# Gated recurrence in a two-part transformer kernel: convolved columns projected first, gate matmuls between the tiles, the elementwise chain in two groups, the output projection by block

## The chip, the core and the metric

The kernel runs on one core of a Trainium2 chip. A core has TensorE (PE in the profile) for matmuls, VectorE (DVE), ScalarE (ACT) and GpSimd (POOL) for elementwise work, and SyncE (SP), which here only issues the loads of weights. Each engine has its own instruction stream; they meet at semaphores. Matmul results go to eight PSUM banks of 128 x 512 float32 values, and a bank can be written again only when another engine has drained it. The metric is the device time of one whole execution in microseconds (us), as the median over the runs.

## The reference, cut to what matters

The model takes 512 tokens of width 1024 through two blocks of two layers each. The change is in one stage, the mixer of the last layer, a gated linear recurrence. `hn` is the normalised input, 512 x 1024.

```python
def rglru_mixer(hn, w_in, conv_w, conv_b, w_a, b_a, w_x, b_x, lam, w_out):
    gate, xr = jnp.split(hn @ w_in, 2, axis=-1)                 # 512 x 1024 each
    xr = (causal_dwconv(xr, conv_w) + conv_b).astype(f32)       # 4 taps
    xb = xr.reshape(b, t, LRU_BLOCKS, LRU_BLOCK)                # 8 blocks of 128
    r = jax.nn.sigmoid(jnp.einsum('btni,nij->btnj', xb, w_a) + b_a)
    i = jax.nn.sigmoid(jnp.einsum('btni,nij->btnj', xb, w_x) + b_x)
    log_a = -LRU_C * r * jax.nn.softplus(-lam)
    a = jnp.exp(log_a)
    u = jnp.sqrt(-jnp.expm1(2.0 * log_a)) * (i * xr)
    _, hs = lax.associative_scan(_linear_combine, (a, u), axis=1)
    y = jax.nn.gelu(gate) * hs
    return y @ w_out
```

Behind it follow the residual, a norm and the convolutional feed-forward layer.

## The kernel before, in words

The kernel is a sequence of stages; the order of the instructions on each engine is written out by hand, and stage 9 is the one of the change. A plan made ahead of the code hands out the eight banks in turn (`plan.take`) and the four weight slots in two pairs (`plan.chunk`): a weight chunk of 1024 x 512 is loaded into one slot of a pair, and its rounded copy goes into the other. The product is made in three matmuls of rounded float32 (`product`): high by high, high by low, low by high. For that ScalarE rounds a chunk in two halves (`round_chunk`), VectorE subtracts the rounded half from the raw one (`rest_of_chunk`), and both have to be done before TensorE uses that half (semaphore `split`). SyncE may load into a slot again only when TensorE has finished the last tile that used it (`c.freed`).

In stage 9 channels lie on the partitions and the 512 tokens in the free dimension. The input projection has 2048 output columns, in four chunks of four tiles of 128 columns; a tile fills one bank with 24 matmuls. The kernel before projects the columns of `gate` first (chunks 0 and 1), which ScalarE takes out of the banks with a Gelu, and the columns of `xr` next (chunks 2 and 3), which VectorE takes out with the convolution (`conv`: one operation and three more, lines 2361 and 2364). The matmuls with the block-diagonal gate weights, two for each of eight tiles, stand behind all of it (line 1926). ScalarE then makes the 16 sigmoids (1347, 1350). After that comes the chain, tile by tile: product i times xr on VectorE (2782), exp, tanh and square on ScalarE (1360, 1362, 1366), the root's argument on VectorE (2788), the root on ScalarE (1370), the product with it on GpSimd (863), the scan over tokens on VectorE (2795), the product with the gate (2797), its rounding on ScalarE (1373) and the rest on VectorE (2802). The output projection waits for all eight tiles:

```python
                pe.wait_ge(signal("lru_y").sem, signal("lru_y").next(pe, KD))
                linear("lru_out")
```

Its stationary operands are XT (rounded) and XH (rest), which were the input of the stage as well: so the chain can't write XT while the input is still being projected.

The names of buffers in the rows: `ring` are the four weight slots, `big` the working area (gate, xr, i, the gate weights w, the squares q), `XT` and `XH` the turned input and its rest, `lnp` a buffer of 2 x 1024 values per partition, `st` and `chan` small tables.

## Time and profile before

| | us |
|---|---|
| median of 3 runs | 3577.34 (3575.35 to 3580.39) |
| profiled execution, its own time | 3585.4 |
| its span, first to last instruction | 3583.6 |
| TensorE busy | 3174.9 (89%) |
| VectorE busy | 2314.3 (65%) |
| ScalarE busy | 1611.3 (45%) |
| GpSimd busy | 412.0 (11%) |

The clock granted to TensorE was 0.936 of the full one in the mean over the span. In the rows, a time at the start is counted from the first instruction; "x8" counts instructions; square brackets, or the last column, hold the idle time of the engine just before, with what ended it. Matmuls overlap, so a duration of 0.39 us is longer than the distance between two starts. In the rows of the trace a float32 gate matmul appears as two records.

### The profile page before, as it was taken

The numbers are of one execution on the slowest core, as the hardware profiler recorded it, in microseconds if no ns is written. First come the engines' busy times: TensorE is split into PE (matmuls) and PEld (weight loads), VectorE is DVE, ScalarE is ACT, GpSimd is POOL, SyncE is SP. The second block draws the span as 40 slices with busy tenths as digits, with TensorE's granted clock in tenths as the row PEclk, the third lists the DMA queues.
The fourth block names the chain that finished last, engine by engine and source line by source line (L and its number), as shares of the span: only waits on it lengthen the run. The fifth ranks groups of instructions, "written<-read, shape, count | busy, mean of one in ns | idle before, by whom it ended". The sixth has DMA issues, their size and how long they took to land.

```text
span 3583.6 us, 40435 instructions
## 1 busy us (share of the span) xinstructions
PE 3174.9 (89%) x15107; PEld 2476.2 (69%) x15107; DVE 2314.3 (65%) x2594; ACT 1611.3 (45%) x1831; POOL 412.0 (11%) x290
## 2 busy tenths in 40 slices
PE   8678699999969999699999969867799998679998
PEld 6456577777758768567767658656678887468886
DVE  2465588888862576778888746466467743657763
ACT  2454277777742353577777632222132213522221
POOL 0000222222220000222222120001100000010000
PEclk9889899999989889799999979888899999889999
DMA  7200499999952003699999844200022222212222
GB/s 262 79 1 12 186 356 346 351 355 357 355 189 94 1 24 113 241 344 349 362 357 361 333 110 99 70 1 1 6 89 94 94 99 78 82 53 94 94 94 82
DMA packets 173509, 597.54 MB, mean 167 GB/s; under 512 B 25491, under 2 KB 74691, under 8 KB 123971
## 3 DMA queue, kind: packets, MB, share of 16 engines
q1 hardware_dynamic: 139552, 539.92, 41.1%
q0 software_dynamic: 23472, 51.42, 4.1%
q10 hardware_dynamic: 10355, 4.42, 0.5%
q8 instruction: 87, 1.43, 0.2%
q14 instruction: 43, 0.35, 0.0%
HBM read 581.01 MB, written 48.23 MB: 176 GB/s over the span
## 4 chain that ended last, share of the span: by engine, by line
PE 76%; DVE 11%; DMA 5%; ACT 3%; issue 3%; POOL 1%; DVEq 0%; SPq 0%; ACTq 0%; POOLq 0%
PE bank L1420 22%; PE bank L1422 21%; PE bank L1421 21%; PE bank L1829 2%; DMA ring<-w_gate 2%; PE bank L1525 2%; PE bank L1602 1%; PE bank L1499 1%; PE bank L1395 1%; DVE st L2093 1%; DVE st L2096 1%; PE bank L1622 1%; DVE big L2090 1%; PE bank L1516 1%; ACT ring_rounded L1021 1%
## 5 line engine op out<-in xcount | busy, mean ns | idle before, releaser
L1421 PE MATMUL bank<-ring_rounded,big_rounded 128*96 128x512 f32 (+1 forms) x1648 | 651.4, 395 | 0.0
L1964 DVE TENSOR_TENSOR ring_rounded<-ring,ring_rounded 128x2048 fp32r<-128x2048 f32 (+2 forms) x128 | 282.5, 2249 | 501.4 <-ACT ring_rounded L901 501.3
L2275 DVE TENSOR_TENSOR ring_rounded<-ring,big_rounded 128x2048 fp32r<-128x2048 f32 x252 | 567.3, 2288 | 42.6 <-ACT big_rounded L1021 41.4
L1021 ACT ACTIVATE big_rounded<-ring 128x2048 fp32r<-128x2048 f32 x252 | 478.0, 1918 | 61.2 <-DMA ring<-w_up 52.7
L901 ACT ACTIVATE ring_rounded<-ring 128x2048 fp32r<-128x2048 f32 (+2 forms) x128 | 234.2, 1880 | 521.1 <-DMA ring<-ffn_w_up 184.8
L1420 PE MATMUL bank<-big_rounded 128*96 128x512 f32 x1008 | 401.1, 398 | 0.0
L1422 PE MATMUL bank<-big_rounded,XH_rounded 128*96 128x512 f32 x1008 | 398.4, 395 | 0.0
L2275 DVE TENSOR_TENSOR ring_rounded<-ring,ring_rounded 128x2048 fp32r<-128x2048 f32 x128 | 292.7, 2288 | 163.0 <-ACT ring_rounded L1021 154.9
L1420 PE MATMUL bank<-ring_rounded,XT_rounded 128*128 128x512 f32 (+1 forms) x864 | 340.4, 394 | 60.6 <-DVE XH_rounded L2802 46.6
L1422 PE MATMUL bank<-ring_rounded,XH_rounded 128*96 128x512 f32 (+1 forms) x944 | 377.3, 400 | 0.0
L1420 PE MATMUL bank<-XT_rounded,ring_rounded 128*128 128x512 f32 x928 | 361.3, 389 | 0.0
L1422 PE MATMUL bank<-XT_rounded,ring_rounded 128*128 128x512 f32 x928 | 361.0, 389 | 0.0
L1421 PE MATMUL bank<-XH_rounded,ring_rounded 128*128 128x512 f32 x928 | 361.0, 389 | 0.0
L1421 PEld LDWEIGHTS bank<-ring_rounded,big_rounded 128*96 128x96 f32 (+1 forms) x1648 | 272.8, 166 | 106.4 <-issue 0.5
L1021 ACT ACTIVATE ring_rounded<-ring 128x2048 fp32r<-128x2048 f32 x128 | 245.1, 1916 | 222.6 <-DMA ring<-w_gate 222.5
L1421 PE MATMUL bank<-ring_rounded,XT_rounded 128*128 128x512 f32 (+1 forms) x864 | 338.3, 392 | 0.0
L1420 PE MATMUL bank<-ring_rounded,big_rounded 128*96 128x512 f32 (+1 forms) x640 | 261.8, 409 | 15.0 <-DVE XH_rounded L2280 7.3
L1422 PE MATMUL bank<-ring_rounded,big_rounded 128*128 128x512 f32 (+1 forms) x672 | 261.8, 390 | 0.0
L1420 PEld LDWEIGHTS bank<-ring_rounded,XT_rounded 128*128 128x128 f32 x864 | 164.3, 190 | 96.0 <-DVE XH_rounded L2802 47.4
L1422 PEld LDWEIGHTS bank<-big_rounded,XH_rounded 128*96 128x96 f32 x1008 | 162.3, 161 | 71.5
L1420 PEld LDWEIGHTS bank<-big_rounded 128*96 128x96 f32 x1008 | 164.8, 164 | 66.3 <-DVE ring_rounded L2275 0.8
L1422 PEld LDWEIGHTS bank<-ring_rounded,XH_rounded 128*96 128x96 f32 (+1 forms) x944 | 166.8, 177 | 55.6 <-issue 0.3
(389 smaller groups left out, 4799.2 us busy)
## 6 DMA issues: line engine op xcount, KB each, us to landing
ring<-w_up SPq DMA_DIRECT2D x128, 1024.0 KB, 7.7
ring<-w_down SPq DMA_DIRECT2D x128, 1024.0 KB, 7.9
ring<-w_gate SPq DMA_DIRECT2D x128, 1024.0 KB, 7.3
ring<-ffn_w_up SPq DMA_DIRECT2D x44, 1024.0 KB, 6.8
ring<-ffn_w_down SPq DMA_DIRECT2D x10, 2048.0 KB, 7.8
ring<-ret_gdn_w_in SPq DMA_DIRECT2D x8, 2048.0 KB, 13.1
expert_rows<-lnp POOLq DMA_DIRECT2D x1, 12288.0 KB, 39.2
ring<-odd_w_qkv SPq DMA_DIRECT2D x6, 2048.0 KB, 8.1
```

Source lines behind the costliest of these rows:

```text
L901: act.activation(one_pass(hi(c)[:, ks, :]), raw(c)[:, ks, :], ACT.Copy).then_inc(rounded[c.pair], 1)
L1021: act.activation(one_pass(expert_hi(j)), expert_raw(j), ACT.Copy).then_inc(signal("half_rounded").sem, 1)
L1395: ins = pe.transpose(ps(u)[:, t * P:(t + 1) * P], src[:, t, i * P:(i + 1) * P], ident)
L1420: pe.matmul(dst, x_hi, y_hi, start=first, stop=False)
L1421: pe.matmul(dst, x_hi, y_lo, start=False, stop=False)
L1422: return pe.matmul(dst, x_lo, y_hi, start=False, stop=last)
L1499: ins = pe.matmul(ps(v)[:, :], buf["QKT"][r, g % 2, 0, t * P:(t + 1) * P], buf["QKT"][r, g % 2, 1, :], start=True, stop=True)
L1516: ins = pe.transpose(ps(v)[:, kt * P:(kt + 1) * P], buf["p"][(i - 2) % 3][:, o, kt * P:(kt + 1) * P], ident)
L1525: ins = pe.matmul(ps(v)[:, 0:c["dv"]], buf["WT"][:, (i - 3) % 2, o, kt, :], c["v"]((i - 3) // T, o, kt), start=(kt == 0), stop=(kt == T - 1))
L1829: ins = pe.matmul(ps(u)[:, i * P:(i + 1) * P], lhsT[:, 2 * q + i, :], rhs[:, 2 * q + i, :], start=True, stop=True)
L1964: dve.tensor_tensor(one_pass(w), w, parts(hi(c)[:, ks, :]), ALU.subtract).then_inc(split[c.pair], 1)
L2275: dve.tensor_tensor(one_pass(expert_raw(j)), expert_raw(j), parts(expert_hi(j)), ALU.subtract).then_inc(signal("half_split").sem, 1)
```

## The change

- The weight columns are loaded in the order 2, 3, 0, 1, so that chunks 0 and 1 are now the columns of xr and chunks 2 and 3 those of gate.
- The gate matmuls stand between tiles of the projection: those of blocks 0 and 1 behind the first tile of chunk 1, of 2 and 3 behind its second, of 4 and 5 behind the first tile of chunk 2, of 6 and 7 behind its second. The plan of banks follows that order.
- The gate weights are loaded earlier, before the turned input is rounded.
- The chain runs in two groups, blocks 0 to 3 and 4 to 7. Its buffer r (sigmoid, tanh, root) is no longer XT but four tiles in lnp; the second group uses them again when the first has been scanned. The product with the root is on VectorE instead of GpSimd.
- Two of the gate tiles are copied out of their banks and put through the Gelu later in place, the other six go through it on the way out. Product with the gate, rounding and rest come last; the results stay in the buffers of xr and i.
- The output projection takes its stationary operands from there and waits for each block by itself in its first tile.

```diff
+LRU_GATES = {(1, 0): (0, 1), (1, 1): (2, 3), (2, 0): (4, 5), (2, 1): (6, 7)}
...
+        for i in range(4):
+            c = plan.chunk(KD, BANK, BANK)
+            us = []
+            for q in range(4):
+                us += plan.take()
+                for m in LRU_GATES.get((i, q), ()):
+                    U["lru"][m] = plan.take(2)
...
+        L_["r"] = lnp[:, :, :].rearrange("p a (b s) -> p (a b) s", b=2)
...
-                load_cols("lru_in", a["lru_w_in_2"][0], 2 * D)
+                load_cols("lru_in", a["lru_w_in_2"][0], 2 * D, order=(2, 3, 0, 1))
...
-                for m in range(KD):
-                    pool.wait_ge(signal("lru_root").sem, signal("lru_root").next(pool))
-                    pool.tensor_tensor(XT[:, m, :], XT[:, m, :], L_["i"][:, m, :], ALU.mult).then_inc(signal("lru_in").sem, 1)
...
+                def sigmoids(ms):
                     for m in ms:
+                        ur, ui = U["lru"][m]
+                        if m >= KD // 2:
+                            act.wait_ge(signal("lru_scanned").sem, signal("lru_scanned").next(act))
...
+                early, last = range(0, KD // 2), range(KD // 2, KD)
+                round_chunk(W["lru_in"][1])
+                round_chunk(W["lru_in"][2])
+                sigmoids(early)
+                act.wait_ge(signal("cvec_ready").sem, signal("cvec_ready").next(act))
+                decays(early)
+                roots(early)
+                round_chunk(W["lru_in"][3])
+                gate_tile(0, ACT.Copy)
+                sigmoids(last[0:2])
+                gate_tile(1, ACT.Copy)
+                sigmoids(last[2:4])
+                decays(last)
+                roots(last)
+                round_chunk(W["lru_out"][0])
+                for m in range(2):
+                    act.activation(L_["gate"][:, m, :], L_["gate"][:, m, :], ACT.Gelu_apprx_tanh).then_inc(signal("lru_gelu").sem, 1)
+                    act.wait_ge(signal("lru_gelu").sem, signal("lru_gelu").next(act))
+                for m in range(2, 6):
+                    gate_tile(m, ACT.Gelu_apprx_tanh)
+                for m in range(4):
+                    round_gated(m)
+                for m in range(6, 8):
+                    gate_tile(m, ACT.Gelu_apprx_tanh)
+                    round_gated(m - 2)
+                for m in range(6, 8):
+                    round_gated(m)
+                round_chunk(W["lru_out"][1])
...
+                    for q in range(4):
+                        linear_T(c, us, range(4), "rms1_T" if i == 0 else None, q)
+                        for m in LRU_GATES.get((i, q), ()):
+                            if m == 0:
+                                pe.wait_ge(signal("gates_loaded").sem, signal("gates_loaded").next(pe, 32))
+                            v = U["lru_in"][m // 4][m % 4]
+                            pe.wait_ge(drained[v.bank], v.n + 1)
+                            for j, u in enumerate(U["lru"][m]):
+                                if u.n:
+                                    pe.wait_ge(drained[u.bank], u.n)
+                                pe.matmul(ps(u)[:, :], L_["w"][:, j, m, :], L_["xr"][:, m, :], start=True, stop=True).then_inc(
+                                    full[u.bank], 1)
...
-                pe.wait_ge(signal("lru_y").sem, signal("lru_y").next(pe, KD))
-                linear("lru_out")
...
+                            if i == 0 and t == 0:
+                                pe.wait_ge(signal("lru_y").sem, signal("lru_y").next(pe))
...
+                rest_of_chunk(W["lru_in"][1])
+                for m in range(5):
+                    lru_conv(m)
+                rest_of_chunk(W["lru_in"][2])
+                for m in range(2):
+                    gated_input(m)
+                lru_conv(5)
+                for m in range(2, 4):
+                    gated_input(m)
+                for m in range(2):
+                    lru_conv(6 + m)
+                    root_argument(2 * m)
+                    root_argument(2 * m + 1)
+                for m in range(4):
+                    recurrence(m)
+                rest_of_chunk(W["lru_in"][3])
+                for m in range(4, 8):
+                    gated_input(m)
+                for m in range(4, 8):
+                    root_argument(m)
+                for m in range(4, 8):
+                    recurrence(m)
+                rest_of_chunk(W["lru_out"][0])
+                for m in range(4):
+                    gated(m)
+                for m in range(4, 8):
+                    rest_of_gated(m - 4)
+                    gated(m)
+                for m in range(4, 8):
+                    rest_of_gated(m)
+                rest_of_chunk(W["lru_out"][1])
```

First the order on TensorE around the first gate matmuls, before the change, with the semaphores each instruction waits for. L1420 to L1422 are the three matmuls of a product, L1926 is a gate matmul; this is the end of the last projected tile.

```order
L1421 MATMUL bank<-XH_rounded,ring_rounded 128x512
L1422 MATMUL bank<-XT_rounded,ring_rounded 128x512
L1926 MATMUL bank<-big 128x512 [waits bank3_drained,gates_loaded]
L1926 MATMUL bank<-big 128x512 [waits bank4_drained]
L1926 MATMUL bank<-big 128x512 [waits bank5_drained,bank4_drained]
L1926 MATMUL bank<-big 128x512 [waits bank6_drained]
L1926 MATMUL bank<-big 128x512 [waits bank7_drained,bank5_drained]
L1926 MATMUL bank<-big 128x512 [waits bank0_drained]
```

Eight more gate matmuls follow, and then the output projection. After the change the first four stand behind the fifth projected tile, with the sixth tile behind them (the product is now L1459 to L1461, a gate matmul L1970):

```order
L1460 MATMUL bank<-XH_rounded,ring_rounded 128x512
L1461 MATMUL bank<-XT_rounded,ring_rounded 128x512
L1970 MATMUL bank<-big 128x512 [waits bank0_drained,bank3_drained,gates_loaded]
L1970 MATMUL bank<-big 128x512 [waits bank1_drained]
L1970 MATMUL bank<-big 128x512 [waits bank2_drained,bank4_drained]
L1970 MATMUL bank<-big 128x512 [waits bank3_drained]
L1459 MATMUL bank<-XT_rounded,ring_rounded 128x512 [waits bank4_drained]
L1460 MATMUL bank<-XH_rounded,ring_rounded 128x512
```

So sixteen gate matmuls in one row became four groups of four, each ahead of a projected tile that now stands behind their waits.

ScalarE in the middle of the stage, before the change: L901 rounds half a chunk, L1336 is a Gelu out of a bank, L1347 and L1350 are the sigmoids.

```order
L1336 ACTIVATE big<-bank 128x512 x4
L901 ACTIVATE ring_rounded<-ring 128x2048 x2
L1336 ACTIVATE big<-bank 128x512 x4
L877 DMA big<-lru_w_a 128x8x128
L877 DMA big<-lru_w_x 128x8x128
L901 ACTIVATE ring_rounded<-ring 128x2048 x4
L1347 ACT_TABLE_LOAD
L1347 ACTIVATE XT<-bank,chan 128x512
L1350 ACTIVATE big<-bank,chan 128x512
```

After the change, the place between the first group's roots (L1373) and the second group's sigmoids (L1348, L1352); L908 rounds the fourth chunk and L1378 takes a gate tile out of its bank.

```order
L1373 ACT_TABLE_LOAD
L1373 ACTIVATE lnp<-lnp 128x512 x4
L908 ACTIVATE ring_rounded<-ring 128x2048 x2
L1378 ACTIVATE big<-bank 128x512
L1348 ACT_TABLE_LOAD
L1348 ACTIVATE lnp<-bank,chan 128x512
L1352 ACTIVATE big<-bank,chan 128x512
L1348 ACTIVATE lnp<-bank,chan 128x512
L1352 ACTIVATE big<-bank,chan 128x512
L1378 ACTIVATE big<-bank 128x512
```

The rounding of the fourth chunk, which needs its load, now stands ahead of the gate tile and the sigmoids of the second group.

VectorE at the end of the stage, before: L2795 is the scan, L2797 the product with the gate, L2802 the rest, L2028 the residual.

```order
L2795 SCALAR_TENSOR_TENSOR big<-big,XT 128x512
L2797 TENSOR_TENSOR big<-big 128x512
L2802 TENSOR_TENSOR XH_rounded<-big,XT_rounded 128x4x128
L2795 SCALAR_TENSOR_TENSOR big<-big,XT 128x512
L2797 TENSOR_TENSOR big<-big 128x512
L2802 TENSOR_TENSOR XH_rounded<-big,XT_rounded 128x4x128 x5
L2028 SCALAR_TENSOR_TENSOR X<-X,bank 128x512 x4
```

After: L2847 is the scan, L2018 the rest of the first output chunk, L2856 the product with the gate, L2861 the rest.

```order
L2845 TENSOR_TENSOR lnp<-lnp,big 128x512
L2847 SCALAR_TENSOR_TENSOR big<-big,lnp 128x512
L2018 TENSOR_TENSOR ring_rounded<-ring,ring_rounded 128x2048 x2
L2856 TENSOR_TENSOR big<-big 128x512 x4
L2861 TENSOR_TENSOR big_rounded<-big,big_rounded 128x512
L2856 TENSOR_TENSOR big<-big 128x512
L2861 TENSOR_TENSOR big_rounded<-big,big_rounded 128x512
L2856 TENSOR_TENSOR big<-big 128x512
L2861 TENSOR_TENSOR big_rounded<-big,big_rounded 128x512
L2856 TENSOR_TENSOR big<-big 128x512
L2861 TENSOR_TENSOR big_rounded<-big,big_rounded 128x512
```

The products with the gate moved from between the scans to behind all of them and behind a weight chunk's rest.

## Rows read from the trace of the kernel before

**Rows 1.** Page, costliest groups: busy, mean ns, idle before.
```profile
L1420 PE MATMUL bank<-ring_rounded,XT_rounded 128*128 128x512 f32 (+1 forms) x864 | 340.4, 394 | 60.6 <-DVE XH_rounded L2802 46.6
```

**Rows 2.** Stretches: length; PE, PEld, DVE, ACT, POOL busy; clock; DMA share, GB/s.
```profile
2400.00:2500.00 100.00, 65.86 (x424) 59.67 (x422) 66.43 (x107) 23.59 (x42) 17.00 (x12) 0.80 0.00 1
3002.00:3089.00 87.00, 87.00 (x389) 72.14 (x387) 41.49 (x51) 27.05 (x26) 0.00 (x0) 1.00 0.26 85
3089.00:3100.00 11.00, 11.00 (x28) 4.93 (x26) 5.82 (x8) 4.22 (x5) 0.00 (x0) 1.00 0.55 191
3100.00:3155.00 55.00, 5.62 (x10) 2.12 (x9) 42.93 (x42) 40.51 (x58) 13.12 (x8) 0.56 0.00 0
```

**Rows 3.** Timeline of TensorE in the stage: start us, duration us.
```profile
3002.54 0.47 PE L1420 MATMUL bank<-XT_rounded,ring_rounded 128*128 128x512 f32 x1
...
3089.69 10.46 PE L1926 MATMUL bank<-big 128*128 128x512 f32 x24
...
3102.95 5.37 PE L1926 MATMUL bank<-big 128*128 128x512 f32 x8 [2.80 <-ACT XT L1347]
3154.90 0.79 PE L1420 MATMUL bank<-ring_rounded,XT_rounded 128*128 128x512 f32 x1 [46.58 <-DVE XH_rounded L2802]
3155.49 0.63 PE L1421 MATMUL bank<-ring_rounded,XT_rounded 128*128 128x512 f32 x1
3155.92 0.63 PE L1422 MATMUL bank<-ring_rounded,XH_rounded 128*128 128x512 f32 x1
...
3199.91 0.39 PE L1422 MATMUL bank<-ring_rounded,XH_rounded 128*128 128x512 f32 x1
```

**Rows 4.** Timeline of VectorE in the stage.
```profile
3009.54 4.49 DVE L1964 TENSOR_TENSOR ring_rounded<-ring,ring_rounded 128x2048 fp32r<-128x2048 f32 x2
...
3062.83 0.81 DVE L2361 TENSOR_SCALAR big<-bank,chan 128x512 f32<-128x512 f32 x1
3063.67 2.32 DVE L2364 SCALAR_TENSOR_TENSOR big<-bank,chan,big 128x511 f32<-128x511 f32 x3
...
3123.72 2.31 DVE L2795 TENSOR_TENSOR_SCAN big<-big,XT 128x512 f32<-128x512 f32 x1 [2.66 <-POOL XT L863]
3126.06 1.58 DVE L2797 TENSOR_TENSOR big<-big 128x512 f32<-128x512 f32 x1
...
3129.36 1.22 DVE L2795 TENSOR_TENSOR_SCAN big<-big,XT 128x512 f32<-128x512 f32 x1
3130.61 0.69 DVE L2797 TENSOR_TENSOR big<-big 128x512 f32<-128x512 f32 x1
...
3151.25 3.60 DVE L2802 TENSOR_TENSOR XH_rounded<-big,XT_rounded 128x512 fp32r<-128x512 f32 x5
```

**Rows 5.** Timeline of ScalarE in the stage.
```profile
3032.75 3.72 ACT L901 ACTIVATE ring_rounded<-ring 128x2048 fp32r<-128x2048 f32 x2 [7.48 <-DMA ring<-lru_w_in]
...
3046.43 0.60 ACT L1336 ACTIVATE big<-bank 128x512 f32<-128x512 f32 x1 [4.84 <-PE bank L1422]
...
3056.47 3.72 ACT L901 ACTIVATE ring_rounded<-ring 128x2048 fp32r<-128x2048 f32 x2 [9.44 <-DMA ring<-lru_w_in]
...
3110.75 1.28 ACT L1360 ACT_TABLE_LOAD   x1
3112.04 0.72 ACT L1360 ACTIVATE big<-XT,st 128x512 f32<-128x512 f32 x1
```

**Rows 6.** ScalarE's instructions by line, 3079 to 3156: busy us, mean ns, idle before.
```profile
L1350 ACT ACTIVATE big<-bank,chan 128x512 f32<-128x512 f32 x8 | 5.5, 687 | 0.6 <-PE bank L1926 0.4
L1360 ACT ACTIVATE big<-XT,st 128x512 f32<-128x512 f32 x8 | 5.7, 710 | 0.0
L1362 ACT ACTIVATE XT<-XT,st 128x512 f32<-128x512 f32 x8 | 5.8, 721 | 0.3
L1366 ACT ACTIVATE big<-big 128x512 f32<-128x512 f32 x8 | 5.0, 629 | 0.3
```

**Rows 7.** DMA issues, 2960 to 3220: size, median us to landing.
```profile
ring<-lru_w_in SPq DMA_DIRECT2D x4, 2048.0 KB, 8.1
```

More of the change, by code:

```diff
@@ L358, in build @@
         U["rms1_T"] = plan.take(KD)
-        plan_linear("lru_in", 2 * D)
-        U["lru"] = [plan.take(2) for _ in range(KD)]
+        W["lru_in"], U["lru_in"], U["lru"] = [], [], [None] * KD
+        for i in range(4):
[5 more added lines that the diff above has]
+                    U["lru"][m] = plan.take(2)
+            plan.freed[c.slot] = ("bank", us[-1])
+            W["lru_in"].append(c)
+            U["lru_in"].append(us)
         plan_linear("lru_out", D)
@@ L1446, in linear_chunk, with linear_T @@
                     ins.then_inc(full[u.bank], 1)
-            def linear_T(c, us, tiles, turned=None):
+            def linear_T(c, us, tiles, turned=None, only=None):
                 for q, (u, m) in enumerate(zip(us, tiles)):
+                    if only is not None and q != only:
+                        continue
                     if u.n:
@@ L1924, in _ @@
+                for i, (c, us) in enumerate(zip(W["lru_out"], U["lru_out"])):
+                    for t, u in enumerate(us):
                         if u.n:
                             pe.wait_ge(drained[u.bank], u.n)
-                        pe.matmul(ps(u)[:, :], L_["w"][:, j, m, :], L_["xr"][:, m, :], start=True, stop=True).then_inc(
-                            full[u.bank], 1)
-                pe.wait_ge(signal("lru_y").sem, signal("lru_y").next(pe, KD))
-                linear("lru_out")
+                        for kk in range(KD):
+                            if t == 0 and kk % 4 == 0:
+                                pe.wait_ge(split[c.pair], 2 * c.nth - 1 + kk // 4)
+                            if i == 0 and t == 0:
+                                pe.wait_ge(signal("lru_y").sem, signal("lru_y").next(pe))
+                            tok = slice(t * P, (t + 1) * P)
+                            ins = product(ps(u)[:, :], L_["xr"][:, kk, tok], L_["i"][:, kk, tok], hi(c)[:, kk, :], raw(c)[:, kk, :], kk == 0, kk == KD - 1)
+                        ins.then_inc(full[u.bank], 1)
```

105 lines of the change are left out of this document (44 added, 61 removed).

## The prediction, made before the changed kernel was run

> **What bounds the kernel now.** I read the page first. TensorE is busy for 3174.9 of 3583.6 us, so only a stretch in which it stands still can give much. The costliest groups show one: the first matmul of a product whose stationary side is XT waited 46.6 us for VectorE's line 2802, the last step of the recurrence [rows 1]. Next the table of stretches: from 3002 to 3100 TensorE is never idle and the clock is granted in full (1.00, the 2.4 GHz level), while in 3100:3155 it has 5.62 us of work [rows 2]. The timeline then gives the frame of the stage: the input projection starts at 3002.54 and ends at 3089.69, the gate matmuls run until 3108.3, and the output projection runs from 3154.90 to 3200.3, where the next stage takes over [rows 3]. These 197.8 us are the stretch that the change can alter. TensorE's own work in it is much shorter; the rest is the elementwise chain (sigmoid, exp, tanh, square, root, scan), which begins only after the last projected tile.
>
> **What TensorE must do, as one number.** A tile of 24 matmuls takes (3089.69 - 3002.54)/16 = 5.45 us, 0.227 a matmul. A gate matmul leaves two records, 24 records take 10.46 us, so one costs 0.87 us and sixteen 13.95 us [rows 3]. The output projection has 192 matmuls, 43.5 us; it took 45.4 because its first ones started 0.43 us apart (the low level, 1.2 GHz, after the long wait) [rows 3]. Without any wait the stage takes 87.15 + 13.95 + 43.5 = 144.6 us, 53.2 less than now. That is the most the change can give, since it removes no matmul.
>
> **The change, part by part.** The order of the weight chunks (xr columns first), the gate matmuls between tiles and the two groups only move work. So the question is whether each wait in the new TensorE order is met in time. I write TensorE's undisturbed times in the clock of this trace: xr tiles 0 to 3 done at 3024.3, tile 4 at 3029.8, gates 0 and 1 at 3033.3, tile 5 at 3038.7, gates 2 and 3 at 3042.2, tiles 6 and 7 at 3053.1; gate column tile 0 at 3058.5, gates 4 and 5 at 3062.0, column tile 1 at 3067.4, gates 6 and 7 at 3070.9, column tiles 2 and 3 at 3081.8, the last chunk at 3103.6, the output projection at 3147.2.
>
> First group. VectorE is done with the second chunk's rest at 3014.0 [rows 4]; a convolution is 0.81 + 2.32 us, with its gaps 3.2 [rows 4], so tiles 0 to 3 are convolved by 3027.5 and tile 4 by 3033.0. Gates 0 and 1 need tiles 0 and 1 (3020.4) at 3029.8: 9 us to spare. ScalarE rounds the third chunk, whose load starts when TensorE has finished the first, as now: 3032.75 to 3036.4 [rows 5]. A table load is 1.28 [rows 5] and a sigmoid 0.69, 0.72 with its gap [rows 6]; sigmoids 0 and 1 end at 3040.5, those of 2 and 3 at 3043.3. The bank of the last matmul of gate 3 wants the first sigmoid (3038.4) at 3041.3: met by 3 us. Exp, tanh and square are 2.03 us a tile [rows 6]. The third square waits for VectorE, which first convolves tile 6 (full at 3047.6); that costs ScalarE about 1.5 us, and the four roots end at 3058.3. The multiplication by the root moves from GpSimd to VectorE, where this trace doesn't show it: a product of the same shape takes 0.69 us, and 1.58 while GpSimd was working [rows 4]. I take 0.69, since GpSimd has nothing left to do here, and 1.22 for the scan for the same reason (2.31 beside GpSimd) [rows 4]. Four tiles then end at 3065.5.
>
> Second group, the tight place. The load of the fourth chunk can start at 3053.1. A load takes 8.1 us in the median [rows 7]; the present fourth one took 10.0 (from the end of the second chunk at 3046.4 to 3056.47) [rows 5], beside the two gate weight loads. Those now go out before the transposed tiles and have some 30 us until the first gate. So ScalarE rounds from 3061.3 to 3065.1, copies column tile 0, loads a table and finishes the sigmoids of tile 4 at 3068.4. TensorE wants the last of these banks at 3070.9: 2.5 us to spare, 0.6 if the load takes 10.0. Roots of the second group end at 3086.4, scans at 3092.4. All that is under the last two chunks, on which TensorE works until 3103.6.
>
> Tail. The rounding of the first output chunk (load from 3081.8) ends on ScalarE at 3093.7, VectorE's rest of it at 3096.9. Gated products and rests go at 0.72 each on VectorE (five rests in 3.60) [rows 4]. The in-place Gelu isn't in the trace; between 0.60 (Gelu out of a bank) and 0.72 (exp) I take 0.63 [rows 5, 6]. By that order lru_y 0 to 7 come at 3100.5, 3102.0, 3103.4, 3104.8, 3106.3, 3107.0, 3107.7 and 3108.4. TensorE now asks for them one block at a time, at 3103.6 and every 0.68 us after: the fifth and the last are just met, some tenths late. I put 0.4 us on that. The last output chunk arrives at 3111.7 and is split by 3118, wanted at 3125.4.
>
> Nothing else is on the path: lnp is free between the squares and the last load, GpSimd loses only its eight products, and the residual and the next stage follow the end of the output projection as before.
>
> ScalarE loads seven tables from the first sigmoid on, where it loaded five. The trace shows such a load at 3110.75 for 1.28 us and the next exp at 3112.04, at once [rows 5]; so I count 1.28. The Trainium skill, in ScalarE: Activation LUTs (What ACT_TABLE_LOAD costs), adds some 1.38 us of drain to each switch. By that rule, an estimate, three switches make the first group 4.1 us later, and with those of the second the last lru_y about 5 us: the time would be some 3530 us. The trace speaks against it.
>
> **Sum.** Before 197.8, after 144.6 + 0.4 = 145.0: 52.8 us less. The profiled execution took 3585.4 us (1.8 around its span) and would take 3532.6. The median of the runs is 3577.3, 8.1 lower; there the same difference gives 3524.5 us.
>
> **Rivals.**
> *Late elementwise work* (0.13). VectorE's operations cost what they cost beside GpSimd (1.58 for 0.69, 2.31 for 1.22 [rows 4]), or loads take 10 us. Loads alone push the tail by 2 to 3 us; the dear operations add 16 x 0.9 = 14 us in the tail and 4 x 2 = 8 before it. TensorE would stand for 10 to 20 us ahead of or inside the output projection: 3535 to 3545. For it: most slacks are a few us. Against it: GpSimd is idle here.
> *It does not do what it says* (0.04). The second group stays behind the last projected tile because one engine's order holds it. Half of the present wait of 46.6 us [rows 1] stays, 23 us: 3548.
> *Slower* (0.03). TensorE waits shortly at the sixteen gate matmuls between the tiles, and the clock stays at the low level. At 0.43 instead of 0.227 us [rows 3], 576 projection matmuls cost 117 us more, the gate matmuls up to 14: 3655. It decides from 52.8/0.203 = 260 matmuls at that level. For it: where TensorE works in short pieces, the granted clock is 0.80 in the mean [rows 2]. Against it: from 3002 to 3100 it changes bank every 5.4 us, then every 0.9, at 1.00 [rows 2], and by my times it never waits there. TensorE: Matmul & The Clock Gate, in the Trainium skill (A second HAM failure mode), warns of small pauses between groups of matmuls when banks are cycled; by that rule the time would be this rival's.
>
> **Chances and range.** 0.80 for the forecast (its own range 3517 to 3532: the runs of one kernel spread by 5 us, and each slack may be missed by a little). Faster by over 0.2% (7 us, about what a measurement of this kernel can tell) holds in all cases but the last: 0.95; within 0.2% 0.02, for a mixture of the last two; slower 0.03. The range takes in most of the late case: 3514 to 3543.
>
> **What would show it.** Right: no idle time of TensorE over 1 us between the first tile and the end of the output projection, a stretch of 145 us at clock 1.00; GpSimd without products; VectorE's scans at 1.22. Wrong: idle time at the third gate column tile (banks of the sigmoids of tile 4), or at the first output tile behind lru_y; or a clock under 1.00 between tiles.

## The result, and the profile after

| | before | changed |
|---|---|---|
| median of the first four runs, us | 3576.35 (3564.93 to 3580.39) | 3529.33 (3524.35 to 3544.72) |
| medians of the later rounds, us | 3581.14 (11 runs) | 3531.99 (6 runs) |
| profiled execution, its own time, us | 3585.4 | 3544.7 |
| span | 3583.6 | 3543.0 |
| TensorE busy | 3174.9 | 3184.5 |
| GpSimd busy | 412.0 | 409.1 |

The change is faster: the ratio is 0.9876 (95% interval 0.9841 to 0.9911), and in the five later rounds 0.9842 (0.9819 to 0.9865). The difference of the medians is 47.0 us, later 49.1 us; the ratios of the medians alone would be 0.987 and 0.986. The prediction was 52.8 us and 3524.5.

GpSimd's total hardly fell, though its eight products (13.12 us in the fourth stretch of [rows 2]) are gone: in the stretches from 500 to 1000 and from 1500 to 2000 us, whose code the change leaves alone, the profile counts 7 us more for it in each (114.95 and 121.95, 115.22 and 122.30).

Below, "the stage" is the time from the first matmul of the input projection to the start of the last residual instruction. It went from 197.9 us (3002.54 to 3200.40) to 146.3 us (3013.32 to 3159.61), 51.6 us less. The last residual instruction before and after:

```profile
3200.40 0.69 DVE L2028 SCALAR_TENSOR_TENSOR X<-X,bank 128x512 f32<-128x512 f32 x1 [4.75 <-PE bank L1422]
```

```profile
3159.61 0.69 DVE L2082 SCALAR_TENSOR_TENSOR X<-X,bank 128x512 f32<-128x512 f32 x1 [4.75 <-PE bank L1461]
```

The whole profiled execution gained only 40.7, because this one came to the stage 10.8 us later; behind the stage both take 383 us. The later 10.8 us are the subject of experiment 8.

TensorE's timeline in the changed kernel, which answers to [rows 3]: start, duration, and in brackets the idle time ahead.

```profile
3013.32 0.47 PE L1459 MATMUL bank<-XT_rounded,ring_rounded 128*128 128x512 f32 x1
...
3078.17 3.59 PE L1970 MATMUL bank<-big 128*128 128x512 f32 x8
3081.20 0.79 PE L1459 MATMUL bank<-XT_rounded,ring_rounded 128*128 128x512 f32 x1
...
3114.26 0.39 PE L1459 MATMUL bank<-ring_rounded,big_rounded 128*128 128x512 f32 x1
...
3116.83 0.50 PE L1459 MATMUL bank<-ring_rounded,big_rounded 128*128 128x512 f32 x1 [0.37 <-DVE big_rounded L2861]
...
3118.38 0.47 PE L1459 MATMUL bank<-ring_rounded,big_rounded 128*128 128x512 f32 x1 [0.58 <-DVE big_rounded L2861]
```

From 3013.32 to 3114.26 there is no wait: 16 tiles and 16 gate matmuls in 100.9 us. The last four gate matmuls (eight records, 3.59 us) stand among the tiles. The wait of 46.6 us for line 2802 [rows 1, 3] is gone; in its place are two short waits for the rest of single blocks (line 2861), 0.37 and 0.58 us, inside the first output tile. The stretches say the same, with the columns of [rows 2]:

```profile
3013.00:3100.00 87.00, 87.00 (x360) 66.76 (x359) 64.76 (x83) 56.25 (x69) 0.00 (x0) 1.00 0.21 73
3100.00:3115.00 15.00, 15.00 (x68) 12.43 (x67) 14.56 (x16) 12.52 (x16) 0.00 (x0) 1.00 0.00 2
3115.00:3160.00 45.00, 43.56 (x190) 34.88 (x188) 19.17 (x20) 12.85 (x14) 2.20 (x6) 1.00 0.28 94
```

The clock is 1.00 throughout; GpSimd has no product left. VectorE (14.56 of 15 us) is full and ScalarE (12.52) nearly so just ahead of the output projection. That is the tail of the chain. VectorE's last four rests:

```profile
3117.54 2.87 DVE L2861 TENSOR_TENSOR big_rounded<-big,big_rounded 128x512 fp32r<-128x512 f32 x4
```

So the last lru_y (the signal that a block of the stationary operand is complete) comes at 3120.41, 107.1 us after the start of the stage, and the stage ends 39.2 us after it.

ScalarE at the place that the prediction called tight, to be read beside [rows 5]:

```profile
3073.00 3.72 ACT L908 ACTIVATE ring_rounded<-ring 128x2048 fp32r<-128x2048 f32 x2 [3.60 <-DMA ring<-lru_w_in]
3076.63 0.57 ACT L1378 ACTIVATE big<-bank 128x512 f32<-128x512 f32 x1
3077.21 1.28 ACT L1348 ACT_TABLE_LOAD   x1
3078.51 0.69 ACT L1348 ACTIVATE lnp<-bank,chan 128x512 f32<-128x512 f32 x1
3079.23 0.69 ACT L1352 ACTIVATE big<-bank,chan 128x512 f32<-128x512 f32 x1
```

It stood 3.60 us for the load of the fourth chunk. The sigmoids of tile 4 were out of their banks at 3079.20 and 3079.92. TensorE needed the first bank for its last gate matmul at about 3080.8 (six records of 0.436 us behind 3078.17) and the second for its next tile at 3081.20, so 1.6 and 1.3 us were to spare. The load had taken 8.9 us, not 8.1:

```profile
3064.04 8.94 DMA ring<-lru_w_in
```

### The profile page after: what moved, and what is told of

It is laid out like the page before. It is cut to its first block, busy times and chain, and to the rows that moved or that the text cites. A ratio compares the mean times of both kernels' runs of the same rounds, so it can differ in the third digit from the quotient of the medians.

```text
span 3543.0 us, 40440 instructions
## 1 busy us (share of the span) xinstructions
PE 3184.5 (90%) x15107; PEld 2484.9 (70%) x15107; DVE 2313.2 (65%) x2602; ACT 1615.3 (46%) x1834; POOL 409.1 (12%) x282
## 4 chain that ended last, share of the span: by engine, by line
PE 77%; DVE 10%; DMA 5%; ACT 3%; issue 3%; POOL 1%; DVEq 0%; SPq 0%; ACTq 0%; POOLq 0%
PE bank L1459 22%; PE bank L1461 21%; PE bank L1460 21%; PE bank L1870 2%; DMA ring<-w_gate 2%; PE bank L1566 2%; PE bank L1540 1%; PE bank L1643 1%; PE bank L1434 1%; PE bank L1557 1%; DVE st L2147 1%; DVE st L2150 1%; PE bank L1663 1%; DVE ring_rounded L2018 1%; ACT ring_rounded L1028 1%
## 5 line engine op out<-in xcount | busy, mean ns | idle before, releaser
L1460 PE MATMUL bank<-ring_rounded,big_rounded 128*96 128x512 f32 (+1 forms) x1712 | 675.0, 394 | 0.0
L2018 DVE TENSOR_TENSOR ring_rounded<-ring,ring_rounded 128x2048 fp32r<-128x2048 f32 (+2 forms) x128 | 282.4, 2248 | 458.4 <-ACT ring_rounded L908 458.2
L908 ACT ACTIVATE ring_rounded<-ring 128x2048 fp32r<-128x2048 f32 (+2 forms) x128 | 234.1, 1879 | 503.2 <-DMA ring<-ffn_w_up 169.0
L1459 PE MATMUL bank<-big_rounded 128*96 128x512 f32 x1008 | 401.2, 398 | 0.1
L1461 PE MATMUL bank<-big_rounded,XH_rounded 128*96 128x512 f32 x1008 | 398.2, 395 | 0.0
L1459 PE MATMUL bank<-XT_rounded,ring_rounded 128*128 128x512 f32 x928 | 362.9, 391 | 0.0
L1461 PE MATMUL bank<-XT_rounded,ring_rounded 128*128 128x512 f32 x928 | 361.0, 389 | 0.0
L1460 PEld LDWEIGHTS bank<-ring_rounded,big_rounded 128*96 128x96 f32 (+1 forms) x1712 | 283.9, 166 | 108.1 <-issue 0.3
L1461 PE MATMUL bank<-ring_rounded,XH_rounded 128*96 128x512 f32 (+1 forms) x880 | 349.9, 398 | 0.0
L1459 PE MATMUL bank<-ring_rounded,XT_rounded 128*128 128x512 f32 (+1 forms) x800 | 314.1, 393 | 14.6 <-DVE ring_rounded L2018 6.9
L1460 PE MATMUL bank<-ring_rounded,XT_rounded 128*128 128x512 f32 (+1 forms) x800 | 312.1, 390 | 0.0
L1459 PE MATMUL bank<-ring_rounded,big_rounded 128*96 128x512 f32 (+1 forms) x704 | 285.6, 406 | 14.6 <-DVE XH_rounded L2334 5.8
L1461 PE MATMUL bank<-ring_rounded,big_rounded 128*128 128x512 f32 (+1 forms) x736 | 286.4, 389 | 0.0
L1461 PEld LDWEIGHTS bank<-big_rounded,XH_rounded 128*96 128x96 f32 x1008 | 162.3, 161 | 71.5
L1459 PEld LDWEIGHTS bank<-big_rounded 128*96 128x96 f32 x1008 | 164.7, 163 | 66.3 <-DVE ring_rounded L2329 0.5
L751 POOL DMA_INDIRECT expert_rows<-big,idx x64 | 98.6, 1541 | 885.5 <-ACT big L1050 830.1
L1460 PEld LDWEIGHTS bank<-XH_rounded,ring_rounded 128*128 128x128 f32 x928 | 174.2, 188 | 37.1 <-issue 1.0
## 6 DMA issues: line engine op xcount, KB each, us to landing
expert_rows<-lnp POOLq DMA_DIRECT2D x1, 12288.0 KB, 39.2
```

The lines of the kernel that those rows point to most:

```text
L751: pool.indirect_dma_start(expert_rows, bass.IndirectOffsetOnAxis(ap=used[0:CAP, e:e + 1], axis=0), M["YE"][0:CAP, e % 2, :], None, bounds_ ...
L908: act.activation(one_pass(hi(c)[:, ks, :]), raw(c)[:, ks, :], ACT.Copy).then_inc(rounded[c.pair], 1)
L1459: pe.matmul(dst, x_hi, y_hi, start=first, stop=False)
L1460: pe.matmul(dst, x_hi, y_lo, start=False, stop=False)
L1461: return pe.matmul(dst, x_lo, y_hi, start=False, stop=last)
L2018: dve.tensor_tensor(one_pass(w), w, parts(hi(c)[:, ks, :]), ALU.subtract).then_inc(split[c.pair], 1)
```

## The experiments

Every run left a profile of its own, so the stage is read to a tenth of a microsecond, whatever the rest of the execution did. The last columns belong to experiment 8: when the stage began, and how long the attention stretch of an earlier stage took (from the last load of `odd_w_qkv` to the first of `odd_w_o`, the same code in all) at which granted clock.

| run | stage | begins | attention stretch | its clock |
|---|---|---|---|---|
| before | 197.9 | 3002.5 | 141.5 | 0.92 |
| changed | 146.3 | 3013.3 | 153.7 | 0.82 |
| 1 by block, on the kernel before | 192.9 | 3016.5 | 153.7 | 0.82 |
| 2 waits for all blocks | 153.1 | 3001.4 | 143.1 | 0.90 |
| 3 product on GpSimd | 147.9 | 2989.7 | 136.1 | 0.96 |
| 4 gates two tiles later | 154.9 | 2989.2 | 136.0 | 0.96 |
| 5 four extra copies | 149.3 | 3002.8 | 138.3 | 0.94 |
| 6 twelve extra copies | 154.2 | 3004.6 | 143.3 | 0.90 |
| 7 idle time used | 144.8 | 3005.5 | 143.3 | 0.90 |
| 8 changed, again | 146.6 | 3004.9 | 141.3 | 0.92 |
| 9 column order alone, on before | 197.9 | 2994.6 | 138.3 | 0.94 |
| 10 second group behind | 176.9 | 2994.1 | 136.1 | 0.96 |

### 1. The blockwise wait alone

```diff
-                pe.wait_ge(signal("lru_y").sem, signal("lru_y").next(pe, KD))
-                linear("lru_out")
...
+                        for kk in range(KD):
...
+                            if i == 0 and t == 0:
+                                pe.wait_ge(signal("lru_y").sem, signal("lru_y").next(pe))
```

> The kernel before, with only the output projection's wait taken apart: each contraction block waits for its own lru_y. 'The stage' is the time from the first matmul of the input projection to the start of the last residual instruction: 197.9 us before, 146.3 us in the changed kernel. My theory (the gain comes from TensorE's order, and the blockwise wait is worth what lies between the first and the last lru_y, less the matmuls that wait in between): TensorE starts when the first rest is done, 11 us earlier, and then stands between blocks, so it saves one tile less its last block, 4.8 us, perhaps 1 us less by a low clock: the stage 193 to 194.5 us. Rival (the blockwise wait is the main part of the gain): the stage under 187 us. Rival (waiting by pieces holds the clock low): the stage 196 or more.

Measured: 192.9 us, 5.0 us saved, just past the expected 193. TensorE's timeline, where the output projection begins:

```profile
3158.05 0.76 PE L1420 MATMUL bank<-ring_rounded,XT_rounded 128*128 128x512 f32 x1 [35.64 <-DVE XH_rounded L2811]
3158.61 0.63 PE L1421 MATMUL bank<-ring_rounded,XT_rounded 128*128 128x512 f32 x1
3159.04 0.63 PE L1422 MATMUL bank<-ring_rounded,XH_rounded 128*128 128x512 f32 x1
3160.68 0.79 PE L1420 MATMUL bank<-ring_rounded,XT_rounded 128*128 128x512 f32 x1 [1.01 <-DVE XH_rounded L2811]
```

It starts after 35.6 us of waiting instead of 46.6, runs one block at the low level (0.63 us each instead of 0.39), and waits again (1.01 us, then twice 1.07). The start is 10.8 us earlier, but what counts is how much of the first tile is left when the last block comes. One tile is the most that a blockwise wait in the first tile can hide.

### 2. The blockwise wait undone

```diff
-                            if i == 0 and t == 0:
-                                pe.wait_ge(signal("lru_y").sem, signal("lru_y").next(pe))
+                            if i == 0 and t == 0 and kk == 0:
+                                pe.wait_ge(signal("lru_y").sem, signal("lru_y").next(pe, KD))
```

> The changed kernel, with the blockwise wait undone: the output projection waits for all eight lru_y at its first matmul. My theory: TensorE is ready for the output projection 6.2 us before the last lru_y (114.26 against 120.4 in its profile), of which the blockwise wait hides all but 1.3 us. So the stage grows from 146.3 to about 151 us, 1 us more if the clock falls in the wait. Rival (the tail is bound by something else, the weights' split): the stage stays within 0.5 us of 146.3.

```profile
3108.61 0.77 PE L1459 MATMUL bank<-ring_rounded,big_rounded 128*128 128x512 f32 x1 [6.08 <-DVE big_rounded L2861]
3109.18 0.63 PE L1460 MATMUL bank<-ring_rounded,big_rounded 128*128 128x512 f32 x1
...
3112.95 0.40 PE L1460 MATMUL bank<-ring_rounded,big_rounded 128*128 128x512 f32 x1
```

The wait is 6.08 us, as worked out (6.2). The stage is 153.1, two more than 151: I had put one microsecond on the low clock behind the wait and it was about two (nine matmuls from 3108.61 on, 0.43 us apart instead of 0.227). So the blockwise wait is worth 6.8 us here and 5.0 in the kernel before.

### 3. The product by the root on GpSimd again

```diff
+                for m in range(KD):
+                    r = L_["r"][:, m % 4, :]
+                    pool.wait_ge(signal("lru_root").sem, signal("lru_root").next(pool))
+                    pool.tensor_tensor(r, r, L_["i"][:, m, :], ALU.mult).then_inc(signal("lru_in").sem, 1)
...
-                    dve.wait_ge(signal("lru_root").sem, signal("lru_root").next(dve))
+                    dve.wait_ge(signal("lru_in").sem, signal("lru_in").next(dve))
...
-                    dve.tensor_tensor(r, r, x, ALU.mult).then_inc(dve_done.sem, 1)
-                    dve.wait_ge(dve_done.sem, dve_done.next(dve))
```

> The changed kernel, with the product by the root on GpSimd again, as before the change. My theory: GpSimd's product (1.3 to 2 us) overlaps the scan of the tile before, and VectorE's operations beside it grow to the 1.58 and 2.31 us seen before; the two nearly cancel in the second group and the stage stays at 146 to 148 us. The rival named in the prediction (VectorE beside GpSimd pays these prices in the path): scans at 2.3 us in each tile, the second group's scans end 4 us later, and the stage is 150 us or more. If the mean of the scan stays at 1.22 us with GpSimd at work, the contention that I read into the rows of before is not there.

The scans of this run, and GpSimd's products: busy us, mean ns, idle before.

```profile
L2850 DVE TENSOR_TENSOR_SCAN big<-big,lnp 128x512 f32<-128x512 f32 x8 | 15.5, 1939 | 2.9 <-POOL lnp L875 2.7
```

```profile
L875 POOL TENSOR_TENSOR lnp<-lnp,big 128x512 f32<-128x512 f32 x8 | 14.3, 1788 | 82.5 <-ACT lnp L1378 82.0
```

In the changed kernel the same two things are both VectorE's:

```profile
L2847 DVE TENSOR_TENSOR_SCAN big<-big,lnp 128x512 f32<-128x512 f32 x8 | 9.8, 1224 | 0.3
...
L2845 DVE TENSOR_TENSOR lnp<-lnp,big 128x512 f32<-128x512 f32 x8 | 5.5, 692 | 1.5 <-ACT lnp L1373 1.3
```

9.8 + 5.5 = 15.3 us there, 15.5 us here for the scans alone: what GpSimd takes off VectorE it takes away again, by making the scans longer (1.94 against 1.22 us). The stage is 1.6 us longer, inside the expected 146 to 148. The contention that [rows 4] showed is real, and the change removes it at no cost. The Trainium skill says in SBUF — State Buffer (Who interferes with whom) that a VectorE instruction with two inputs in SBUF contends with a GpSimd instruction that reads there. This run agrees: the scans, with two such inputs, take 1.94 us in the mean beside GpSimd and 1.22 without.

### 4. The gate matmuls two tiles later

```diff
-LRU_GATES = {(1, 0): (0, 1), (1, 1): (2, 3), (2, 0): (4, 5), (2, 1): (6, 7)}
+LRU_GATES = {(1, 2): (0, 1), (1, 3): (2, 3), (2, 2): (4, 5), (2, 3): (6, 7)}
...
+                lru_conv(5)
+                lru_conv(6)
+                for m in range(4):
+                    gated_input(m)
```

(The third gate tile is copied out as well and put through the Gelu in place.)

> The changed kernel, with the four pairs of gate matmuls two tiles (10.9 us) later: behind the third and fourth tile of the second chunk, and of the third. One more gate tile is copied out and put through the Gelu in place, and VectorE's convolutions of tiles 5 and 6 come ahead of the first products, since the banks ask for it. My theory (the chain, and not TensorE, is at its limit; its start is the first gate pair): sigmoids of tiles 0 to 3 end at 50.7 instead of 41.0 us after the start of the stage, the first roots 8.5 us later, all of the second group about 8.4 us later, TensorE waits for lru_y that long: the stage 153 to 156 us. Rival (there is slack in the chain and only the order within the last chunk counts): the stage under 149 us.

```profile
3089.88 0.79 PE L1460 MATMUL bank<-XT_rounded,ring_rounded 128*128 128x512 f32 x1 [5.07 <-ACT big L1378]
...
3099.77 0.50 PE L1460 MATMUL bank<-ring_rounded,big_rounded 128*128 128x512 f32 x1 [0.48 <-DVE big_rounded L2862]
```

154.9 us, as the first theory said; of 10.9 us by which the gates come later, 8.6 appear in the stage. Where TensorE waits was not as I wrote: 5.07 us for a bank with a gate tile still in it (line 1378), ahead of the last projected tile, and only the rest at the output projection (three waits, 1.56 us in all, one of them shown). The chain's delay is the same; the banks hand it on sooner.

### 5 and 6. ScalarE delayed at the tight place

```diff
                 round_chunk(W["lru_in"][3])
+                for _ in range(4):
+                    act.activation(L_["q"][:, 0, :], L_["q"][:, 1, :], ACT.Copy).then_inc(act_done.sem, 1)
+                    act.wait_ge(act_done.sem, act_done.next(act))
                 gate_tile(0, ACT.Copy)
```

(`range(12)` in the second run.)

> The changed kernel, with four extra ScalarE copies of 128x512 (about 0.63 us each, 2.6 in all) between the rounding of the fourth chunk and the first gate tile; they write the unused square buffer. The prediction gave this place 2.5 us to spare. In the profile of the changed kernel the last of the banks was drained at 3081.36 and TensorE could use it at 3081.76, so only 0.4 us. Theory A (0.4 us to spare): TensorE stands about 2.2 us at the third gate column tile, and the stage is 148.5 to 149.2 us. Theory B (2.5 us to spare): no wait in the middle, but the chain ends 2.6 us later and the output projection waits so much longer; the stage is about the same, 148.9 us. The place of the wait tells them apart, not the time.

> The same with twelve extra copies, 7.7 us. Theory (chain and TensorE are balanced, every us of ScalarE in this place is a us of the stage): the stage 153.5 to 155 us, with 7.3 us of waiting at the third gate column tile, and after it some matmuls at the low clock (up to 9 of them, 1.8 us), which the chain covers or not. Rival (the chain had several us to spare behind this place): the stage under 151 us. Rival of the prediction (a wait between tiles holds the clock low for long): more than 20 matmuls at a distance of 0.43 us, and the stage 160 us or more.

With four copies:

```profile
3069.72 1.10 PE L1973 MATMUL bank<-big 128*128 128x512 f32 x2 [0.24 <-ACT big L1378]
3071.62 1.13 PE L1973 MATMUL bank<-big 128*128 128x512 f32 x2 [0.81 <-ACT lnp L1348]
...
3106.31 0.50 PE L1462 MATMUL bank<-ring_rounded,big_rounded 128*128 128x512 f32 x1 [0.21 <-DVE big_rounded L2864]
3107.77 0.50 PE L1462 MATMUL bank<-ring_rounded,big_rounded 128*128 128x512 f32 x1 [0.48 <-DVE big_rounded L2864]
```

149.3 us, three more than without. TensorE stands 0.24 + 0.81 = 1.05 us at the last gate matmuls, and 1.76 us in the first output tile (four waits, two of them shown). Neither theory gave the middle wait. Theory A was worked out from a misread row: the bank drained at 3081.36 is that of tile 5, which by the plan of banks is needed only two tiles later. The right rows are those in the result above, 1.3 us to spare ahead of the next tile. Counted from the start of the stage, the sigmoids of tile 4 come 2.9 us later here (2.6 for the copies, 0.3 because the rounding started that much later), and TensorE's next tile starts 1.7 us later: 2.9 less 1.3 is 1.6. The prediction's 2.5 us would have left 0.4.

With twelve copies:

```profile
3076.53 3.98 PE L1973 MATMUL bank<-big 128*128 128x512 f32 x4 [5.17 <-ACT big L1378]
3079.53 1.42 PE L1462 MATMUL bank<-XT_rounded,ring_rounded 128*128 128x512 f32 x1
3080.74 0.63 PE L1463 MATMUL bank<-XH_rounded,ring_rounded 128*128 128x512 f32 x1
...
3082.00 0.39 PE L1463 MATMUL bank<-XH_rounded,ring_rounded 128*128 128x512 f32 x1
```

154.2 us, 7.9 more for 7.7 us of copies. The main wait is at the bank of the first gate tile, ahead of the last two gate matmuls, and not at the third column tile. After 5.17 us of it those two and the first few of the next tile run at the low level, until 3082; nothing holds the clock low for long. Both runs say that ScalarE and TensorE are in step: a microsecond of ScalarE in the middle is about a microsecond of the stage.

What carries the delay to the end is the last lru_y. Counted from the start of the stage it comes at 107.1 us in the changed kernel, 107.4 in experiment 8, 108.7 in 3, 115.65 in 4, 110.0 and 115.0 with the copies and 137.7 in 10, and in all seven profiles the stage ends 39.2 us after it. Where TensorE waited before that makes no difference to the end.

### 7. ScalarE's idle time used

```diff
-                round_chunk(W["lru_in"][3])
                 gate_tile(0, ACT.Copy)
                 sigmoids(last[0:2])
+                round_chunk(W["lru_in"][3])
                 gate_tile(1, ACT.Copy)
...
-                round_chunk(W["lru_out"][0])
...
-                for m in range(2, 6):
+                for m in range(2, 4):
+                    gate_tile(m, ACT.Gelu_apprx_tanh)
+                round_chunk(W["lru_out"][0])
+                for m in range(4, 6):
                     gate_tile(m, ACT.Gelu_apprx_tanh)
...
-                rest_of_chunk(W["lru_out"][0])
                 for m in range(4):
                     gated(m)
+                rest_of_chunk(W["lru_out"][0])
```

> The changed kernel, with ScalarE's idle time used: the first gate tile and the sigmoids of tiles 4 and 5 ahead of the rounding of the fourth chunk (ScalarE stands 3.6 us there for its load), Gelus of gate tiles 0 to 3 ahead of the rounding of the first output chunk (3.7 us idle there), and on VectorE the first four gated products ahead of that chunk's rest. Theory (the last 1.3 us over TensorE's own work are the chain's): sigmoids 3 to 4 us earlier, the bank for the third gate column tile free more than 3 us ahead, lru_y of all blocks ahead of TensorE, the stage 144.9 to 145.3 us instead of 146.3. Rival (the tail is held by the load of the first output chunk, which only TensorE's progress starts): the stage 146 us or more. In the whole time, 1.4 us cannot be told: the ratio to the kernel before as for the changed kernel, 0.985 to 0.990.

```profile
3060.21 1.36 ACT L1373 ACTIVATE lnp<-lnp 128x512 f32<-128x512 f32 x2 [0.24 <-DVE lnp L2840]
3061.65 0.60 ACT L1378 ACTIVATE big<-bank 128x512 f32<-128x512 f32 x1
3062.95 1.28 ACT L1348 ACT_TABLE_LOAD   x1 [0.70 <-DVE big L2849]
...
3066.41 0.69 ACT L1352 ACTIVATE big<-bank,chan 128x512 f32<-128x512 f32 x1
3067.13 3.72 ACT L908 ACTIVATE ring_rounded<-ring 128x2048 fp32r<-128x2048 f32 x2
```

The time that ScalarE stood before the fourth chunk now holds the first gate tile and the sigmoids of tiles 4 and 5. TensorE has no wait left in the whole stage:

```profile
3005.00:3151.00 146.00, 145.13 (x615) 114.58 (x613) 98.95 (x119) 81.56 (x99) 2.20 (x6) 1.00 0.22 72
```

The stage is 144.8 us, 1.5 less than the changed kernel, which is TensorE's own work (the prediction worked it out as 144.6). The last lru_y comes at 105.4 us instead of 107.1. What each of the three moves gives was not taken apart. In whole executions the 1.5 us can't be told: the median of its four runs is 3532.2, the ratio to the kernel before 0.9853 (0.9831 to 0.9874), beside 0.9842 (0.9819 to 0.9865) for the changed kernel in the same rounds. So in the total it beats the kernel before, but can't be told from the changed kernel; in the stage it beats both.

### 8. The changed kernel again

No edit.

> The changed kernel again, timed against the kernel before in five rounds. In its first profile the stage was 51.6 us shorter but the whole only 40.6, since what lies ahead of the stage took 10.8 us longer. Theory (that is a difference from run to run in code that is the same in both): the stage again 146 to 147 us, the part ahead of it back near 3002 us or spread by several us, the ratio 0.9850 to 0.9870 and the difference of the medians 47 to 54 us. Rival (the change itself lengthens something ahead of the stage, as by the placement of code or buffers): the part ahead of the stage 10 us longer again, and the ratio 0.988 or more.

The stage is 146.6 us and begins at 3004.9. The code ahead of it is the same in all twelve profiles but for the early loads of the gate weights, and it takes 2989 to 3016 us. The table above shows where most of that comes from: the attention stretch takes 136.0 to 153.7 us, and it goes with the granted clock, 0.96 to 0.82. The first profile of the changed kernel and experiment 4 have the two ends. Columns as in [rows 2].

```profile
1137.20:1290.90 153.70, 144.14 (x743) 114.30 (x741) 83.86 (x166) 56.85 (x110) 0.00 (x0) 0.82 0.04 14
```

```profile
1136.50:1272.50 136.00, 125.16 (x744) 98.69 (x742) 83.87 (x166) 56.86 (x109) 0.00 (x0) 0.96 0.05 16
```

The same instructions, VectorE and ScalarE busy for the same 83.9 and 56.9 us; TensorE is busy 19 us longer at the lower mean clock. Experiments 1 to 4 ran on one and the same chip and have 136.0 to 153.7 us, so it is not a difference between chips. So the rival that the change lengthens something ahead of the stage falls: experiments 3, 4 and 10 carry the change or most of it and come to the stage 8 to 13 us earlier than the profile of the kernel before. What makes the clock come out differently from run to run in the same code stays open.

### 9. The order of the columns alone

```diff
-                load_cols("lru_in", a["lru_w_in_2"][0], 2 * D)
+                load_cols("lru_in", a["lru_w_in_2"][0], 2 * D, order=(2, 3, 0, 1))
...
-                    for m, u in enumerate(U["lru_in"][2 + i]):
+                    for m, u in enumerate(U["lru_in"][i]):
```

(The second edit is VectorE's convolution; ScalarE's Gelus and the roundings and rests of the chunks follow the new order, and the gate weights are loaded early.)

> The kernel before, with one part of the change alone: xr columns projected and convolved first, gate columns second, gate weights loaded early. The gate matmuls stay behind all projected tiles, the chain stays in XT, in one piece, ahead of the output projection. Theory (the order by itself gives nothing, since the first sigmoids still wait for gate matmuls behind the last tile and ScalarE still stands before the last output chunk's load): the stage 197 to 199 us, as before (197.9). Rival (the convolutions were what held the chain, and their going out of the way is part of the gain): 190 us or less.

```profile
3146.94 0.80 PE L1421 MATMUL bank<-ring_rounded,XT_rounded 128*128 128x512 f32 x1 [46.58 <-DVE XH_rounded L2802]
```

197.9 us, and the same wait of 46.58 us as in [rows 3]. The convolutions were never in the way.

### 10. The second group behind the last tile

```diff
-LRU_GATES = {(1, 0): (0, 1), (1, 1): (2, 3), (2, 0): (4, 5), (2, 1): (6, 7)}
+LRU_GATES = {(1, 0): (0, 1), (1, 1): (2, 3), (3, 3): (4, 5, 6, 7)}
...
-                gate_tile(0, ACT.Copy)
-                sigmoids(last[0:2])
-                gate_tile(1, ACT.Copy)
-                sigmoids(last[2:4])
+                for m in range(8):
+                    gate_tile(m, ACT.Gelu_apprx_tanh)
+                sigmoids(last)
```

(The in-place Gelus go, and all roundings of the gated products come behind the first output chunk's.)

> The changed kernel, with the gate matmuls of blocks 4 to 7 behind the last projected tile; so the first group still runs beside the projection, the second starts behind it, and all gate tiles go through the Gelu on their way out. Theory (worked out with the durations of the changed kernel's profile): second sigmoids end 102 us after the start of the stage, roots 114, scans 122, with the first output chunk's rest the last lru_y at 137.7, and the output projection ends 38 us later: the stage 176 us, 30 us over the changed kernel. The prediction priced this case, as a rival, at half of the old wait, 23 us: the stage 169 us. Rival (the first group's place is what counts, and the second group costs little): under 160 us.

```profile
3123.95 0.77 PE L1448 MATMUL bank<-ring_rounded,big_rounded 128*128 128x512 f32 x1 [28.77 <-DVE big_rounded L2847]
```

176.9 us against 176 worked out. The second group's place among the tiles is worth 30.6 us. The rest of the way to the kernel before, 21 us, is the first group's place, together with what this run keeps of the change: the blockwise wait, the buffers and the product on VectorE.

## Why the prediction was right, and where it was not exact

**The frame and TensorE's own work.** The 144.6 us were right: experiment 7, without a wait, has 144.8. The projection with its gate matmuls took 100.9 us (101.1 worked out), and the clock was 1.00.

**The mechanism.** Right, and shown by parts. The order of the columns alone gives 0.0 us (experiment 9), the blockwise wait alone 5.0 (1), and with the second group left behind, 30.6 of the 51.6 us are missing (10). The gain is that both groups of the chain lie beside projected tiles. Delaying ScalarE or the gate pairs brings the time back (4 to 6).

**The term that was off.** The tail: I put 0.4 us on the waits at the first output tile. They were 0.37 + 0.58 = 0.95 us, and with restarts the stage is 1.5 us longer than in experiment 7. Most of the reason is upstream. The load of the fourth chunk took 8.94 us where the median of 8.1 was used, so ScalarE's rounding started 0.9 us later than worked out (3073.0 in its trace, 3072.1 from the prediction's 3061.3 moved by 10.8). The last lru_y came 1.2 us later than worked out (3120.41, against 3119.2 from its 3108.4); the other 0.3 us came in on the way, by the end of the second group's scans. The long load was no chance: in experiments 3, 5, 6 and 8 that load took 9.03, 9.23, 8.87 and 9.19 us. The slack at the sigmoids of tile 4 was 1.3 instead of 2.5 us: they came 0.7 us late, and TensorE's next tile starts 0.5 us earlier than the sum of times had it, since records overlap. Sum: 51.6 us in place of 52.8.

**The product moved to VectorE.** Right at 0.69 us, and the scans at 1.22 (experiment 3 shows the other side). The prediction's late rival would have needed these at their GpSimd price. Its other condition, a load of 10 us, was nearly met at 8.94, and that cost about a microsecond.

**The table loads.** Seven loads at 1.28 us, each followed at once by the next activation (3077.21 + 1.28, next 3078.51). The further 1.38 us of drain that the Trainium skill gives in ScalarE: Activation LUTs (What ACT_TABLE_LOAD costs) don't show here, neither ahead of the load (the copy before it ends at 3077.20) nor behind it.

**The second group behind, as a rival.** It didn't happen, but its price was put too low: 23 us by halving the wait; experiment 10 costs 30.6. The second group alone keeps TensorE waiting for 28.77 us, well over half of 46.58; halving the wait was a guess that no row supported.

**The slow rival.** The clock stayed at 1.00 in the stage. The low level does come where TensorE waits longer: 0.63 us a matmul in experiment 1, behind 35.64 us of waiting and between waits of 1.0 us, and 0.82 to 0.96 in the mean over the attention stretch. TensorE: Matmul & The Clock Gate of the Trainium skill (A second HAM failure mode) warns of small pauses between groups of matmuls. The stage does not bear that out for its own pauses, 0.37 and 0.58 us at 1.00. Whether such pauses are what lowers the clock in the attention stretch no run here tests.

**The total.** 3529.3 for 3524.5 predicted; 1.2 us of the difference are the stage. The rest is within what the code ahead of the stage does from run to run: its end moves by 27 us between the twelve profiles.

## What to carry to other kernels

When TensorE waits once and long for an elementwise chain, look for matmuls behind or ahead of it that don't need the chain's result, and feed the chain from the middle of them; then write out for every bank the time at which it is wanted and at which it is free, because the smallest of these differences is what a late load eats. Measure such a change in the stage, by its own start and end in the trace: here the whole execution moved by more than 20 us for reasons outside. Once the engines are in step, look for the idle time that is left ahead of a load in an in-order engine, and put there what needs no load.

## What the runs showed of the hardware that was not expected

- The granted clock of one and the same stretch of code differs from run to run, 0.82 to 0.96 in the mean, and the stretch took 136.0 us at the one and 153.7 at the other. These 17.7 us are most of the 27 us by which the start of the stage differs between profiles.
- A wait of about 6 us ahead of dense matmuls (experiment 2) cost 8.3 us against experiment 7, which has no wait: the nine matmuls after it ran at the low level (0.63 us instead of 0.39), for 4 us instead of 2. Behind waits of 0.4 to 0.6 us the level did not change.
- Eight products on GpSimd, 14.3 us in all, lengthened VectorE's scans beside them by 5.7 us (1.94 for 1.22 us each), as much as the products cost on VectorE itself (5.5 us).
